# Token-major MLP up units with moving weights, and a turn of the squared rows on TensorE

## The chip, the cores and the metric

The kernel runs on one core of one Trainium2 chip. The metric is the device time of one execution in microseconds. The kernel before takes 2461.74 us (median of 3 runs, 2461.24 to 2465.61).

## What is computed

Two decoder layers over 256 tokens of width 2048, in float32. Layer 0 mixes tokens by attention, layer 1 by a short convolution; each is followed by an MLP of width 8192. Every part is normalised, shifted and scaled, and added back through a gate. The change concerns the MLP alone:

```python
def sq_relu_mlp(h, w_up, w_down):
    return jnp.square(jax.nn.relu(h @ w_up)) @ w_down

for i in range(DEPTH):                       # DEPTH = 2
    ...
    h = modulate(rmsnorm(x, norm_mlp[i]), sh_mlp, sc_mlp)
    x = x + g_mlp[:, None, :] * sq_relu_mlp(h, mlp_w_up[i], mlp_w_down[i])
return rmsnorm(x, final_norm)
```

## The kernel before

**Units.** All large products are cut into units: a 2048 by 512 block of a weight, multiplied with all 256 tokens. A unit has 16 blocks of 128 rows (k), taken as 8 pairs (e = 0 to 7). Each operand is held as two parts in a short float format (fp32r), the rounded value ("hi") and what is left ("lo"), and each product is three matmuls: hi·hi, hi·lo and lo·hi.

**Two ways to multiply a pair.** `chan_pair` (L383) keeps the weight stationary and lets the tokens move: 2 k-blocks by 4 column blocks by 3 products, 24 matmuls of 128x256 (L392 to L394). Channels come out on the partitions, which is how the next product wants them. `tok_pair` (L397) keeps the tokens stationary and lets the weight move: 2 k-blocks by 2 token blocks by 3 products, 12 matmuls of 128x512 (L404 to L406). Tokens come out on the partitions. Up units use `chan_pair`; down units, the value units of the attention and the output projections use `tok_pair`.

**The MLP.** Each layer goes through 4 slices. A slice has 4 up units, whose squared results fill `mid` (16 k-blocks), and 4 down units that multiply `mid`. Slices 1 and 2 of a layer are one loop run twice. There are 32 up units and 32 down units in all. Units alternate between PSUM banks 0, 1 and banks 2, 3; banks 4 to 7 are used by norms, by attention and (bank 7) by the sums of the conditioning vector.

**Queues.** SP loads `raw` a quarter unit at a time. ScalarE rounds it to `w_hi` (`split`, L674), VectorE subtracts to `w_lo` (L1039), both four pairs ahead of TensorE in a ring of four; ScalarE's rounding of step i waits until TensorE has used pair i. Each engine runs its program in order: `body` and `pairs` walk the 8 steps of a unit and call hooks after given steps. In layer 0 VectorE also does the conditioning products `ada` between its steps (L1051), one weight tile per 16 steps, fed by POOL's loads, and TensorE sums each finished tile (`ada_sum`, L440 or L437): two sums in the up units and two in the down units of a slice.

**After an up unit** ScalarE runs `hidden` (L947): Relu out of PSUM into `scratch` (L955, frees the banks), Square in place (L957), Copy to the hi part of `mid` (L959). VectorE's `low_hidden` (L1437) subtracts to the lo part at L1439, after step 0 of the next unit. The first down unit waits for each fourth of `mid` (`mid_chunks`) before its pairs 0, 2, 4 and 6.

**The first unit of a layer's MLP** runs while the norm is still finishing: after each of pairs 0 to 5 TensorE turns 4 blocks of 128x128 (`turn_pair`, L611), and ScalarE and VectorE make the next pair of `h` from them (L924, L762, L1352, L1149), the splits of the weights lying between.

Of the kernel before, what the change touches and what calls it, by code (L numbers as in the profile page):

```python
# [7 lines left out]
ACT = mybir.ActivationFunctionType  # L8
# [3 lines left out]
P = 128  # L12
D = 2048
T = 256
# [9 lines left out]
TT = T // P  # L24
NU = 512
NB = NU // P
NG = D // NU
# [5 lines left out]
SLICES = FF // D  # L33
# [56 lines left out]
def build(nc, x, c, ada_w, ada_b, norm_mix, norm_mlp, fox_w_in, fox_b_f, fox_w_out,  # L90
          conv_w_in, conv_w, conv_w_out, mlp_w_up, mlp_w_down, final_norm, out):
    ctx = ExitStack()
    with ctx:
# [3 lines left out]
        def sem(name):  # L97
            return ctx.enter_context(nc.semaphore(name))
# [18 lines left out]
        mid = sb("mid", [P, KC, 2, T], F32R)  # L117
# [3 lines left out]
        h = sb("h", [P, KC, 2, T], F32R)  # L121
# [13 lines left out]
        scratch = sb("scratch", [P, 2, TT, NU])  # L135
# [6 lines left out]
        ident = sb("ident", [P, P])  # L142
# [27 lines left out]
        ps = ctx.enter_context(nc.psum_tensor("ps", [P, 8, NU], F32))  # L170
# [38 lines left out]
        evacuated = [sem(f"evacuated{i}") for i in range(2)]  # L209
# [31 lines left out]
        added = sem("added")  # L241
        relu = sem("relu")
        relu2 = sem("relu2")
        hid_hi = sem("hid_hi")
        hid_ready = sem("hid_ready")
        conv_zero = sem("conv_zero")
# [132 lines left out]
        def _(pe):  # L379
            mm = nc.tensor.matmul  # L380
            turn = nc.tensor.transpose
# [27 lines left out]
            def pairs(un, src, multiply=chan_pair, ready=None, after=None, es=range(NE)):  # L409
                for e in es:  # L410
                    if e == 0 and not (isinstance(un.u, int) and un.u < 2):
                        pe.wait_ge(evacuated[un.par], un.before)
                    pe.wait_ge(split_ready, NE * un.u + e + 1)
                    if ready is not None:
                        ready(e)
                    multiply(un, e, src).then_inc(split_used, 1)
                    if after is not None and e in after:
                        after[e]()
# [25 lines left out]
            def sums(table, first, n, is_gate, extra=None):  # L444

                hooks = {}
                for e in range(NE):
                    calls = []
                    if NE * n + e in table:
                        i = table[NE * n + e]  # L450
                        calls.append(lambda i=i: ada_sum(first + i, i % 2, is_gate(i)))
                    if extra is not None and e in extra:
                        calls.append(extra[e])
                    if calls:
                        hooks[e] = lambda calls=calls: [f() for f in calls]
                return hooks
# [43 lines left out]
            def h_chunks(i):  # L500
                return lambda e: pe.wait_ge(h_ready, NE * i + e + 1)
# [84 lines left out]
            for u in range(1, 3 * NG):  # L586
                g, t = u // 3, u % 3
                if t == 0:
                    extra = {2: lambda: mix_values(g - 1)}
                elif t == 1:  # L590
                    extra = None if g else {0: forget_logits, 4: forget_turn, 6: forget_sums}
                else:
                    extra = {1 if g else 2: lambda: scores(g), 7: lambda: turn_probs(g)}
# [5 lines left out]
            for n in range(NG):  # L599
                hooks = sums(QKV_SUM, A_START, U_OUT0 + n, qkv_gate, None if n else {2: lambda: mix_values(NG - 1)})  # L600
# [22 lines left out]
            def next_pair(i):  # L623
                return {e: (lambda e=e: turn_pair(i, e + 2)) for e in range(NE - 2)}


            def mlp_slice(base, s, l, first_ada=None, is_gate=False, norm_i=None):
                for n in range(2 * NG):
                    un = at_mlp(base, s, n)
                    extra = next_pair(norm_i) if norm_i is not None and n == 0 else None  # L630
                    hooks = extra if first_ada is None else sums(SLICE_SUM, first_ada, n, lambda i: is_gate, extra)
                    if n < NG:
                        pairs(un, h, ready=h_chunks(norm_i) if norm_i is not None and n == 0 else None, after=hooks)
                        continue
                    ready = mid_chunks(hid_ready, NG * SLICES * l + NG * s) if n == NG else None
                    if n == 2 * NG - 1:
                        by_block(un, mid, after=hooks)
                    else:
                        pairs(un, mid, tok_pair, ready=ready, after=hooks)
# [9 lines left out]
            for i in range(3 * NG):  # L649
                pairs(at(U_CONV + i), h, ready=None if i else h_chunks(2),  # L650
                      after=sums(CONV_SUM, A_CONV, i, lambda i: i < NG, None if i else next_pair(2)))
            for n in range(NG):
                hooks = sums(CONV_SUM, A_CONV, 3 * NG + n, lambda i: i < NG)
# [11 lines left out]
        def _(act):  # L665
# [17 lines left out]
            def body(un, first=None, after=None, last=False):  # L683
                for i in range(NE):
                    if first is not None and i in first:
                        first[i]()
                    if i < WR or not last:
                        split(un.u, i)
                    if after is not None and i in after:
                        after[i]()  # L690
# [242 lines left out]
            def load_gate(layer, part, n_added):  # L933
                act.wait_ge(added, n_added)
                act.dma_start(gate[:, :], ada_b[layer:layer + 1, D * part:D * (part + 1)].broadcast_to([P, D])
                              ).then_inc(gate_arrived, 16)
# [10 lines left out]
            def hidden(un, n, hid, n_added):  # L947

                half = scratch[:, n % 2, :, :]
                flat_half = half.rearrange("p a n -> p (a n)").rearrange("p (j t) -> p j t", j=NB)  # L950
                done(un)
                act.wait_ge(added, n_added)
                if n >= 2:
                    act.wait_ge(hid_ready, hid - 1)
                op(flat_half, un.chan(), ACT.Relu).then_inc(evacuated[un.par], 1)  # L955
                act.wait_ge(evacuated[un.par], un.before + 1)
                op(half, half, ACT.Square).then_inc(relu2, 1)  # L957
                act.wait_ge(relu2, hid + 1)
                op(mid[:, NB * n:NB * (n + 1), 0, :], flat_half, ACT.Copy).then_inc(hid_hi, 1)  # L959

            def mlp_slice(base, s, l, norm_before=None, gate_part=None, norm_after=None, last=False):
                hid = SLICES * NG * l + NG * s
                r0 = (R_MLP0, R_MLP1)[l] + NG * s
                for n in range(NG):
                    un = at_mlp(base, s, n)
                    hooks = {7: lambda: hidden(un, n, hid + n, r0)}
                    if n == 0 and norm_before is not None:
                        hooks.update(rest_of_norm(norm_before))
                        hooks[5] = lambda: load_gate(l, gate_part, r0)
                    body(un, None, hooks)  # L970
                for n in range(NG):
                    final = None
                    if last and n == 0:
                        final = {0: load_final}
                    residual(at_mlp(base, s, NG + n), n, r0, norm_after, final, last=last and n == NG - 1)

            def load_final():
# [54 lines left out]
        def _(dve):  # L1032
# [404 lines left out]
            def low_hidden(n, hid):  # L1437
                dve.wait_ge(hid_hi, hid + 1)
                v.tensor_tensor(mid[:, NB * n:NB * (n + 1), 1, :],  # L1439
                                scratch[:, n % 2, :, :].rearrange("p a n -> p (a n)").rearrange("p (j t) -> p j t", j=NB),  # L1440
                                mid[:, NB * n:NB * (n + 1), 0, :].bitcast(F32), ALU.subtract).then_inc(hid_ready, 1)

            def mlp_slice(base, s, l, i0=None, store=None, norm_before=None, norm_after=None, last=False):
                hid = SLICES * NG * l + NG * s
                r = (R_MLP0, R_MLP1)[l] + NG * s
                for n in range(2 * NG):
                    un = at_mlp(base, s, n)
                    extra = {}
                    if n == 0 and norm_before is not None:
                        extra = rest_of_norm(norm_before)  # L1450
                    if 0 < n <= NG:
                        extra[0] = lambda: low_hidden(n - 1, hid + n - 1)
                    if last and n > NG:
                        extra[1] = lambda: output(n - NG - 1)
                    hooks = extra if store is None else stores(SLICE_STORE, n, store, extra)
                    steps = None if store is None else PLAN_SLICE[0][n]
                    if n < NG:
                        body(un, None, hooks, steps, i0)
                    else:
                        residual(un, n - NG, r, norm_after, hooks, steps, i0, last=last and n == 2 * NG - 1)  # L1460
# [81 lines left out]
```

## Time and profile before

| | |
|---|---|
| median of 3 runs | 2461.74 us (2461.24 to 2465.61) |
| the profiled execution | 2466.71 us, of which its span 2464.7 us |
| TensorE matmul busy | 95% of the span, 15235 matmuls |
| VectorE busy | 69% |
| ScalarE busy | 43% |
| mean granted TensorE clock | 0.972 |
| DMA | 616 MB, 250 GB/s |

A row of a group gives the line, the engine and the operation, what is written and read, the count, the busy time in us and the mean of one in ns. Matmuls are pipelined, so one lasts longer than the distance from start to start, which is what it costs. The timeline gives the start in us from the span's start, and the length.

### The profile page before, as it was taken

What the parts mean: (1) busy time and instruction counts of PE and PEld (TensorE: products, weight loads), DVE (VectorE), ACT (ScalarE), POOL (GpSimd) and SP (SyncE); (2) the same over time, 40 slices, a digit from 0 to 9 for tenths busy, and PEclk for the clock granted to TensorE, in tenths of its full rate; (3) what the DMA queues carried; (4) which work ended last, traced back from release to release, by engine and by line L of the source; (5) the groups of instructions that cost most, each with busy time, mean ns of one, the idle gap of its engine ahead of it and who ended that gap; (6) DMA issues with size and microseconds to landing.
All of it is one profiled execution on the core that took longest, in us unless ns stands there. A gap on an engine that the chain in (4) does not pass through costs nothing.

```text
span 2464.7 us, 36963 instructions
## 1 busy us (share of the span) xinstructions
PE 2352.1 (95%) x15235; PEld 2162.1 (88%) x15235; DVE 1692.3 (69%) x1936; ACT 1051.7 (43%) x1179; POOL 123.9 (5%) x176
## 2 busy tenths in 40 slices
PE   6789999998999999999998999998999999999998
PEld 6779999778989989989988998986998997998996
DVE  5857778886886775776776777765787555455455
ACT  4134434435534533534445333344543443443443
POOL 0000000000000000000000000000000000000000
PEclk9689999999999999999999999999999999999999
DMA  9966778885886886886885788775687555555563
GB/s 364 361 219 222 274 280 301 283 313 183 304 299 228 304 299 211 305 297 227 304 300 164 274 299 290 276 239 169 222 315 248 184 181 190 181 185 189 190 205 120
DMA packets 267568, 616.17 MB, mean 250 GB/s; under 512 B 11672, under 2 KB 12040, under 8 KB 266512
## 3 DMA queue, kind: packets, MB, share of 16 engines
q1 hardware_dynamic: 219968, 437.29, 52.5%
q0 software_dynamic: 43520, 167.78, 18.7%
q10 hardware_dynamic: 3920, 8.75, 1.0%
q8 instruction: 126, 2.06, 0.3%
q14 instruction: 34, 0.28, 0.0%
HBM read 611.66 MB, written 2.13 MB: 249 GB/s over the span
## 4 chain that ended last, share of the span: by engine, by line
PE 85%; DVE 7%; ACT 3%; DMA 2%; issue 2%; SPq 0%; ACTq 0%; DVEq 0%
PE ps L392 16%; PE ps L393 15%; PE ps L394 15%; PE ps L404 11%; PE ps L406 11%; PE ps L405 11%; DVE acc L1051 2%; DMA ada_raw<-in_ada_w_dram 2%; DVE w_lo L1039 2%; ACT w_hi L674 1%; DMA start_ring<-in_ada_w_dram 1%; PE ps L440 1%; PE ps L471 1%; PE ps L437 1%; ACT scratch L820 1%
## 5 line engine op out<-in xcount | busy, mean ns | idle before, releaser
L1039 DVE TENSOR_TENSOR w_lo<-raw,w_hi 128x1024 fp32r<-128x1024 f32 x768 | 938.3, 1223 | 614.0 <-ACT w_hi L674 610.5
L674 ACT ACTIVATE w_hi<-raw 128x1024 fp32r<-128x1024 f32 x760 | 802.9, 1059 | 1180.8 <-PE ps L394 645.7
L392 PE MATMUL ps<-h,w_hi 128*128 128x256 f32 x3328 | 960.8, 289 | 12.2 <-DVE h L1149 9.0
L393 PE MATMUL ps<-h,w_hi 128*128 128x256 f32 x3328 | 951.4, 286 | 2.4 <-issue 2.4
L394 PE MATMUL ps<-h,w_lo 128*128 128x256 f32 x3328 | 950.7, 286 | 0.0
L392 PEld LDWEIGHTS ps<-h,w_hi 128*128 128x128 f32 x3328 | 649.0, 195 | 17.8 <-issue 16.1
L393 PEld LDWEIGHTS ps<-h,w_hi 128*128 128x128 f32 x3328 | 649.1, 195 | 5.3 <-issue 5.1
L394 PEld LDWEIGHTS ps<-h,w_lo 128*128 128x128 f32 x3328 | 648.6, 195 | 0.0
L404 PE MATMUL ps<-w_hi,mid 128*128 128x512 f32 x1280 | 503.1, 393 | 0.0
L405 PE MATMUL ps<-w_hi,mid 128*128 128x512 f32 x1280 | 498.7, 390 | 0.0
L406 PE MATMUL ps<-w_lo,mid 128*128 128x512 f32 x1280 | 498.6, 390 | 0.0
L1051 DVE SCALAR_TENSOR_TENSOR acc<-ada_raw,ca,acc 128x512 f32<-128x512 f32 x600 | 448.6, 748 | 26.0 <-DMA ada_raw<-in_ada_w_dram 18.5
L405 PEld LDWEIGHTS ps<-w_hi,mid 128*128 128x128 f32 x1280 | 240.7, 188 | 51.5 <-issue 2.2
L404 PEld LDWEIGHTS ps<-w_hi,mid 128*128 128x128 f32 x1280 | 240.8, 188 | 51.1 <-issue 1.2
L406 PEld LDWEIGHTS ps<-w_lo,mid 128*128 128x128 f32 x1280 | 240.6, 188 | 50.3
L373 POOL DMA_DIRECT2D ada_raw<-in_ada_w_dram x160 | 120.0, 750 | 1744.1 <-DVE acc L1051 1713.2
L1051 DVE SCALAR_TENSOR_TENSOR acc<-start_ring,ca,acc 128x512 f32<-128x512 f32 x88 | 66.1, 751 | 6.5 <-DMA start_ring<-in_ada_w_dram 3.7
L471 PE MATMUL ps<-ca,start_ring 128*128 128x1 f32 x256 | 46.8, 312 | 13.4 <-DMA start_ring<-in_ada_w_dram 7.8
L471 PEld LDWEIGHTS ps<-ca,start_ring 128*128 128x128 f32 x256 | 46.7, 280 | 14.0 <-DMA start_ring<-in_ada_w_dram 8.2
L404 PE MATMUL ps<-w_hi,h 128*128 128x512 f32 x128 | 50.3, 393 | 0.0
L405 PE MATMUL ps<-w_hi,h 128*128 128x512 f32 x128 | 49.9, 390 | 0.0
L406 PE MATMUL ps<-w_lo,h 128*128 128x512 f32 x128 | 49.9, 390 | 0.0
(166 smaller groups left out, 985.4 us busy)
## 6 DMA issues: line engine op xcount, KB each, us to landing
ada_raw<-in_ada_w_dram POOLq DMA_DIRECT2D x160, 1024.0 KB, 7.3
raw<-in_mlp_w_up_dram SPq DMA_DIRECT2D x128, 1024.0 KB, 5.4
raw<-in_mlp_w_down_dram SPq DMA_DIRECT2D x128, 1024.0 KB, 5.2
raw<-in_fox_w_in_dram SPq DMA_DIRECT2D x48, 1024.0 KB, 5.5
raw<-in_conv_w_in_dram SPq DMA_DIRECT2D x48, 1024.0 KB, 6.1
start_ring<-in_ada_w_dram SPq DMA_DIRECT2D x32, 1024.0 KB, 10.7
raw<-in_fox_w_out_dram SPq DMA_DIRECT2D x16, 1024.0 KB, 6.6
raw<-in_conv_w_out_dram SPq DMA_DIRECT2D x16, 1024.0 KB, 5.2
```

The costliest lines, as they stand in the source:

```text
L373: pool.dma_start(ada_raw[:, t % 2], ada_quarter(A_START + t // NQ, t % NQ)).then_inc(ada_arrived[t % 2], 16)
L392: mm(o, hi[:, jc], xh, start=(k == 0 and j % 2 == 0), stop=False, skip_group_check=True)
L393: mm(o, hi[:, jc], xl, start=False, stop=False, skip_group_check=True)
L394: last = mm(o, lo[:, jc], xh, start=False, stop=(k == KC - 1), skip_group_check=True)
L404: mm(o, xh, hi, start=(k == 0), stop=False)
L405: mm(o, xl, hi, start=False, stop=False)
L406: last = mm(o, xh, lo, start=False, stop=(k == KC - 1))
L437: last = mm(ps[:, SUM, :], ones[:, :], acc[:, slot, :], start=True, stop=True)
L471: last = mm(ps[:, 6 + i % 2, j:j + 1], start_ring[:, t % RING, k % QK, P * j:P * (j + 1)], ca[:, k:k + 1], start=(k == START_DVE and j == ...
L674: op(w_hi[:, e % WR], raw[:, e // 2, EK * (e % 2):EK * (e % 2 + 1)], ACT.Copy).then_inc(hi_ready, 1)
L1039: v.tensor_tensor(w_lo[:, e % WR], raw[:, e // 2, EK * (e % 2):EK * (e % 2 + 1)], w_hi[:, e % WR].bitcast(F32), ALU.subtract).then_inc(spl ...
L1051: v.scalar_tensor_tensor(acc[:, slot, :], src, ca[:, col:col + 1], acc[:, slot, :], ALU.mult, ALU.add).then_inc(steps, 1)
```

## The change

Up units call `tok_pair` in place of `chan_pair`, so that tokens come out on the partitions. ScalarE's Relu and Square work on that layout. TensorE then turns the squared rows, 8 blocks of 128x128, into banks 4 and 5 (`turn_hidden`), in the next unit after pair 2. ScalarE rounds the hi part of `mid` out of those banks (`round_hidden`), and VectorE subtracts its lo part out of them, both after step 3 of the next unit in place of straight after the Square and after step 0. `scratch` is free again once it is turned, so `hidden` waits for `hid_turned`. `turn_hidden` waits for the Square (`relu2`) and for the lo part of the unit before (`hid_ready`).

```diff
+            def turn_hidden(n, hid):
+
+                pe.wait_ge(relu2, hid + 1)
+                pe.wait_ge(hid_ready, hid)
+                for j in range(NB):
+                    for a in range(TT):
+                        last = turn(ps[:, 4 + j // 2, T * (j % 2) + P * a:T * (j % 2) + P * (a + 1)],
+                                    scratch[:, n % 2, a, P * j:P * (j + 1)], ident[:, :])
+                last.then_inc(hid_turned, 1)
+
             def mlp_slice(base, s, l, first_ada=None, is_gate=False, norm_i=None):
                 for n in range(2 * NG):
                     un = at_mlp(base, s, n)
                     extra = next_pair(norm_i) if norm_i is not None and n == 0 else None
+                    if 0 < n <= NG:
+                        extra = {2: lambda: turn_hidden(n - 1, NG * SLICES * l + NG * s + n - 1)}
                     hooks = extra if first_ada is None else sums(SLICE_SUM, first_ada, n, lambda i: is_gate, extra)
                     if n < NG:
-                        pairs(un, h, ready=h_chunks(norm_i) if norm_i is not None and n == 0 else None, after=hooks)
+                        pairs(un, h, tok_pair, ready=h_chunks(norm_i) if norm_i is not None and n == 0 else None, after=hooks)
                         continue
...
                 half = scratch[:, n % 2, :, :]
-                flat_half = half.rearrange("p a n -> p (a n)").rearrange("p (j t) -> p j t", j=NB)
                 done(un)
                 act.wait_ge(added, n_added)
                 if n >= 2:
-                    act.wait_ge(hid_ready, hid - 1)
-                op(flat_half, un.chan(), ACT.Relu).then_inc(evacuated[un.par], 1)
+                    act.wait_ge(hid_turned, hid - 1)
+                op(half, un.tok(), ACT.Relu).then_inc(evacuated[un.par], 1)
                 act.wait_ge(evacuated[un.par], un.before + 1)
                 op(half, half, ACT.Square).then_inc(relu2, 1)
-                act.wait_ge(relu2, hid + 1)
-                op(mid[:, NB * n:NB * (n + 1), 0, :], flat_half, ACT.Copy).then_inc(hid_hi, 1)
+
+            def round_hidden(n, hid):
+                act.wait_ge(hid_turned, hid + 1)
+                op(mid[:, NB * n:NB * (n + 1), 0, :], ps[:, 4:6, :].rearrange("p b (j t) -> p (b j) t", t=T),
+                   ACT.Copy).then_inc(hid_hi, 1)
...
+                    if n:
+                        hooks[3] = lambda: round_hidden(n - 1, hid + n - 1)
...
+                    if n == 0:
+                        final[3] = lambda: round_hidden(NG - 1, hid + NG - 1)
...
             def low_hidden(n, hid):
                 dve.wait_ge(hid_hi, hid + 1)
                 v.tensor_tensor(mid[:, NB * n:NB * (n + 1), 1, :],
-                                scratch[:, n % 2, :, :].rearrange("p a n -> p (a n)").rearrange("p (j t) -> p j t", j=NB),
+                                ps[:, 4:6, :].rearrange("p b (j t) -> p (b j) t", t=T),
                                 mid[:, NB * n:NB * (n + 1), 0, :].bitcast(F32), ALU.subtract).then_inc(hid_ready, 1)
...
                     if 0 < n <= NG:
-                        extra[0] = lambda: low_hidden(n - 1, hid + n - 1)
+                        extra[3] = lambda: low_hidden(n - 1, hid + n - 1)
```

## Rows read from the trace of the kernel before

**Rows 1.** The page: engine totals over the span, and the chain that ended last.
```profile
PE 2352.1 (95%) x15235; PEld 2162.1 (88%) x15235; DVE 1692.3 (69%) x1936; ACT 1051.7 (43%) x1179; POOL 123.9 (5%) x176
PE 85%; DVE 7%; ACT 3%; DMA 2%; issue 2%; SPq 0%; ACTq 0%; DVEq 0%
```
**Rows 2.** Stretches: length, busy us (count) by engine, granted clock, DMA share, GB/s.
```profile
1960.05:1983.09 23.04, 23.04 (x194) 23.04 (x193) 10.85 (x9) 11.39 (x12) 0.00 (x0) 1.00 0.57 184
...
617.78:665.56 47.78, 47.78 (x386) 46.60 (x385) 37.94 (x43) 22.83 (x24) 4.49 (x6) 1.00 0.89 313
...
1724.50:1729.80 5.30, 5.26 (x25) 5.29 (x26) 3.71 (x5) 1.81 (x4) 0.00 (x0) 0.50 0.03 3
...
31.00:47.00 16.00, 14.53 (x71) 14.47 (x71) 13.18 (x18) 8.99 (x13) 0.00 (x0) 1.00 1.05 387
```
**Rows 3.** Waits of TensorE, 590 to 1200 us and 1830 to 2380 us.
```profile
PE ps L393 <- issue: 2.4, 1, 2.4
```
```profile
PE ps L392 <- issue: 2.5, 1, 2.5
```
**Rows 4.** Timeline of ScalarE in an up unit, then in a down unit.
```profile
1996.53 1.06 ACT L674 ACTIVATE w_hi<-raw 128x1024 fp32r<-128x1024 f32 x1 [1.82 <-PE ps L394]
1999.41 1.06 ACT L674 ACTIVATE w_hi<-raw 128x1024 fp32r<-128x1024 f32 x1 [1.82 <-PE ps L394]
...
2016.07 1.06 ACT L674 ACTIVATE w_hi<-raw 128x1024 fp32r<-128x1024 f32 x1 [1.66 <-PE ps L406]
2018.79 1.06 ACT L674 ACTIVATE w_hi<-raw 128x1024 fp32r<-128x1024 f32 x1 [1.66 <-PE ps L406]
```
**Rows 5.** Timeline of TensorE, layer 1's first up unit: the matmuls that follow four turns.
```profile
1736.85 0.36 PE L392 MATMUL ps<-h,w_hi 128*128 128x256 f32 x1
...
1740.16 0.36 PE L392 MATMUL ps<-h,w_hi 128*128 128x256 f32 x1
```
**Rows 6.** Timeline of TensorE in the attention: twelve turns in a row.
```profile
206.39 0.27 PE L566 MATMUL ps<-ident,scratch 128*128 128x128 f32 x1
...
207.49 0.31 PE L567 MATMUL ps<-ident,scratch 128*128 128x128 f32 x1
207.51 0.50 PE L392 MATMUL ps<-h,w_hi 128*128 128x256 f32 x1
```
**Rows 7.** Timeline of TensorE at the start: eight turns of x.
```profile
33.28 1.94 PE L496 MATMUL ps<-ident,scratch 128*128 128x128 f32 x8 [1.47 <-ACT scratch L741]
```
**Rows 8.** Timeline of TensorE in a down unit: eight sums between pairs.
```profile
919.33 0.95 PE L440 MATMUL ps<-ones,acc 128*128 128x1 f32 x8
920.13 0.49 PE L404 MATMUL ps<-w_hi,mid 128*128 128x512 f32 x1
920.46 0.40 PE L405 MATMUL ps<-w_hi,mid 128*128 128x512 f32 x1
```
**Rows 9.** Timeline of VectorE and ScalarE, layer 1's first up unit, from one pair of h to the next.
```profile
1744.57 0.54 DVE L1352 TENSOR_SCALAR hb<-ps,gain,mod 128x256 f32<-128x256 f32 x1
...
1746.76 1.23 DVE L1039 TENSOR_TENSOR w_lo<-raw,w_hi 128x1024 fp32r<-128x1024 f32 x1 [0.26 <-ACT w_hi L674]
1747.90 0.54 DVE L1352 TENSOR_SCALAR hb<-ps,gain,mod 128x256 f32<-128x256 f32 x1
```
```profile
1745.14 0.63 ACT L762 ACTIVATE h<-hb 128x512 fp32r<-128x512 f32 x1 [0.77 <-DVE hb L1352]
1745.68 1.04 ACT L674 ACTIVATE w_hi<-raw 128x1024 fp32r<-128x1024 f32 x1
```
**Rows 10.** Groups by line, ScalarE and VectorE.
```profile
L1039 DVE TENSOR_TENSOR w_lo<-raw,w_hi 128x1024 fp32r<-128x1024 f32 x768 | 938.3, 1223 | 614.0 <-ACT w_hi L674 610.5
L1051 DVE SCALAR_TENSOR_TENSOR acc<-ada_raw,ca,acc 128x512 f32<-128x512 f32 x600 | 448.6, 748 | 26.0 <-DMA ada_raw<-in_ada_w_dram 18.5
...
L1239 DVE TENSOR_TENSOR mid<-ps,mid 128x1024 fp32r<-128x1024 f32 x4 | 4.9, 1218 | 0.0
...
L830 ACT ACTIVATE mid<-ps 128x1024 fp32r<-128x1024 f32 x4 | 4.0, 1008 | 0.0
```

More of the change, by code:

```diff
@@ L243, in build @@
         relu2 = sem("relu2")
+        hid_turned = sem("hid_turned")
         hid_hi = sem("hid_hi")
@@ L969, in mlp_slice @@
                         hooks[5] = lambda: load_gate(l, gate_part, r0)
+                    if n:
+                        hooks[3] = lambda: round_hidden(n - 1, hid + n - 1)
                     body(un, None, hooks)
                 for n in range(NG):
-                    final = None
+                    final = {}
+                    if n == 0:
+                        final[3] = lambda: round_hidden(NG - 1, hid + NG - 1)
                     if last and n == 0:
-                        final = {0: load_final}
+                        final[0] = load_final
                     residual(at_mlp(base, s, NG + n), n, r0, norm_after, final, last=last and n == NG - 1)
```

## The prediction

> **What bounds the kernel now.** I read the engine totals first, then the chain that ended last, then stretches of single units, and last the timeline inside them. TensorE is busy in 95% of the span and carries 85% of the chain [rows 1]. An average over stages doesn't say what a unit is bound by, so the stretches decide: an up unit of layer 1 lasts 23.04 us with TensorE busy for all 23.04, VectorE for 10.85 and ScalarE for 11.39; two up units of layer 0 last 47.78 us with TensorE busy for 47.78 and VectorE for 37.94 [rows 2]. TensorE's only wait in each MLP loop is one of 2.4 to 2.5 us, at the jump back [rows 3]. So in the MLP the time is the number of TensorE instructions by their distance from start to start. What the others do is free as long as it stays inside their slack.
>
> The distance is read from ScalarE, whose split starts each time TensorE has used a pair: 2.88 us for a pair of an up unit, 2.72 us for a pair of a down unit [rows 4]. That is 24 matmuls of 256 columns at 120 ns, and 12 of 512 columns at 227 ns. The columns at 2.4 GHz would take 106.7 and 213.3 ns, so either kind carries 13.3 ns beside its columns, and the up unit pays it twice as often. 8 x 2.88 = 23.04 is the whole unit.
>
> **The matmuls.** The up units change from 24 to 12 matmuls per pair over the same columns. Down units have exactly the new form, and the value units of the attention have it with the same stationary `h`, so I take 2.72 us: 0.16 us less per pair, 1.28 us per unit. It would be 41.0 us for 32 units, if each were bound by TensorE.
>
> Two aren't, the first unit of each layer's MLP. There a chain passes through VectorE's modulation (starts 1744.57), ScalarE's rounding of h (1745.14), ScalarE's split (1745.68), VectorE's split (1746.76) and the next modulation (1747.90): 3.33 us around [rows 9], against 3.31 us that TensorE takes for a pair and four turns (1736.85 to 1740.16) [rows 5]. Taking 0.16 us from TensorE leaves the 3.33. I give these two units 0.2 us each, for the pairs after the last turn; the bounds are 0 and 1.28. Saved: 30 x 1.28 + 2 x 0.2 = 38.8 us.
>
> **The turns.** 32 x 8 turns are added, all on the engine that bounds. Three rows bound them. Four turns between pairs of the same MLP cost 3.31 - 2.88 = 0.43 us, the restart of the matmuls included [rows 4, 5]. In a row of twelve, ten steps take 1.10 us, 0.11 each, and the first matmul follows the last turn by 0.02 [rows 6]. Eight then cost 0.43 + 4 x 0.11 = 0.87 us. At the kernel's start eight took 1.94 us [rows 7]. I take the low end, because its rows lie in the very stage that is changed. Matmuls of 512 columns surround them now. After eight short sums in a down unit the second matmul follows the first by 0.33 us where 0.227 is usual, 0.10 lost in the restart [rows 8]; part of such a loss is in the 0.43 already. I add 0.02 us (bounds 0 and 0.10). So 0.89 us, and 32 x 0.89 = 28.5 us. An up unit becomes 8 x 2.72 + 0.89 = 22.65 us in place of 23.04.
>
> A rule of the Trainium skill speaks against this, in the page "TensorE: Matmul & The Clock Gate", Part 4 (PE-mode transpose): a transpose in a kernel's context takes about 275 ns. As an estimate by that page, eight would be 2.2 us, a unit 0.92 us slower than before, and the kernel 2491 us. The trace doesn't agree as to distance: the rows show 0.11 us from turn to turn.
>
> **The sums of layer 0.** Eight of them lie in up units whose matmuls are now long: the restart after them loses up to the same 0.10 us more than it did [rows 8]. I book 0.5 us in all (0 to 0.8).
>
> **ScalarE.** The Copy to `mid` is of the same size and reads PSUM now, which takes 1008 ns [rows 10], so nothing is added, and it moves from the end of the unit to after step 3. Its split of step 0 comes 1 us earlier. ScalarE is half idle (11.39 of 23.04), which hides all of it. Its new wait (`hid_turned` before the rounding) stands behind split 3, which itself waits until TensorE has finished pair 3; the turns come before pair 3 in TensorE's order, so it is met by then. Nothing queues behind it.
>
> **VectorE.** The subtraction is of the same size and reads PSUM: 1218 ns [rows 10]. It moves from step 0 to step 3. In layer 0 VectorE is busy for 37.94 of 47.78 us; that becomes about 38 of 47.0. It stays under TensorE.
>
> **The new waits on TensorE.** `turn_hidden` waits for the Square. That is done about 3.1 us after the unit's end (a split, the Relu and the Square, about 1.05 us each by rows of this size [rows 4, 10]), and the turns are due after three pairs, 8.2 us. 5 us are left. It also waits for the lo part of the unit before, done a unit ago. Queued behind are pairs 3 to 7, with the ring of splits four pairs ahead.
>
> The last up unit of a slice is the tight one, since the first down unit needs its lo part before pair 6. From that unit's start: pair 3 ends at 4 x 2.72 + 0.89 = 11.8; ScalarE's split ends at 12.8 and its rounding at 13.8; VectorE's split ends at 14.1 and the lo part at 15.3; pair 6 starts at 6 x 2.72 + 0.89 = 17.2. Slack 1.9 us in layer 1. In layer 0 up to two conditioning steps of 0.75 us can stand ahead, which leaves 0.4. Before, the lo part came after step 0. So the change costs nothing here, but has little to spare.
>
> **DMA, SP and POOL** get no new transfer. The rate rises by 1.7% at most where TensorE is faster; the DMA share was 0.89 in the densest units [rows 2]. Loads of `raw` are issued about 6 pairs (16 us) ahead of their split. Free, with the smallest reserve in layer 0.
>
> **The loop's jump.** Two waits of 2.4 to 2.5 us for instructions stay [rows 3]. Before them now stand matmuls that run longer, which could hide 0.3 us of each; I book nothing.
>
> **Where the clock is low** (0.50 granted in the stretch after the norm [rows 2], which is the level of 1.2 GHz), 25 instructions fill 5.3 us: 213 ns for 256 columns, no more than the columns. The short form pays nothing there, so the long one gains nothing. That concerns one or two pairs per norm, already outside the sum.
>
> **The sum.** -38.8 + 28.5 + 0.5 = -9.8 us. The profiled execution took 2466.71 us (span 2464.7 and 2.0 around it); it becomes about 2456.9. It stood 5.0 us above the median of the runs, within what a few more microseconds of low clock can do. From the median: 2461.7 - 9.8 = 2451.9, I say 2452 us.
>
> **Rivals.**
> A, the slower one: a turn costs what it did at the start, 1.94 us for eight [rows 7]. For it: that stretch has 1.00 in the clock column [rows 2], so the row isn't excused by the clock; and nothing shows turns of `scratch` between 512-column matmuls. Against: the turns of [rows 5, 6] ran at 0.11. It decides above 1.28 / 8 = 0.16 us per turn. Time: 2461.7 - 38.8 + 62.1 + 0.5 = 2485.5 us.
> B, also slower: the 13.3 ns isn't a cost per matmul in the up units, so that a long one there takes 2 x 120 ns. Then nothing is saved: 2461.7 + 28.5 + 0.5 = 2490.7 us. Against: the long matmuls of the down units keep 227 ns [rows 4]. A page of the Trainium skill comes out near this by another road: "TensorE: Matmul & The Clock Gate", Back-to-back issue gap, gives N / 2.4 + 2.5 ns. As an estimate by it, a pair would shrink by 0.03 us only, and the kernel would take about 2483 us. The 120 and 227 ns of this trace disagree with it by 11 ns each, and the measurement decides.
> C: the fourth chunk comes late. It eats more than its 0.4 us in layer 0's four slices by one or two VectorE instructions (0.75 to 1.22 us): 2452 + 4 x 1.5 = 2458 us.
> D: the change doesn't reach layer 0, because VectorE's and DMA's load there sets the pace once TensorE is faster. Only 16 units gain: 2457 us. Against: 38 of 47.0 us.
> E: instruction waits or stretches of low clock fall otherwise, 3 to 8 us more: 2455 to 2460 us.
>
> **How the numbers follow.** Forecast 0.78 (own range 2447 to 2456), C 0.05, D 0.06, E 0.04, A 0.04, B 0.03. About 0.2% (4.9 us) is what a measurement of this kernel can tell from no change, so faster means below 2456.8. Forecast and half of E give 0.80 faster; C, D and the rest of E 0.13; A and B 0.07. The range reaches from 2446 (all 32 units gain in full, turns 0.86, part of the jump hidden) to 2460 (C, D and E); A and B are left out.
>
> **What the profile after should show.** Splits in up units 2.72 us apart; 8 turns from pair 2 to pair 3 taking 0.89 us; layer 1's units 22.65 us from Relu to Relu; 15235 - 32 x 96 + 256 = 12419 matmuls; no wait of TensorE for `mid` in a first down unit. A turn above 0.16 us, pairs above 2.77 us, or a wait before pair 6 would make me wrong.

## The result and the profile after

The changed kernel takes 2440.37 us (median of 4 runs, 2438.44 to 2442.30) beside 2461.97 us of the kernel before: ratio 0.9914, 95% interval 0.9897 to 0.9931. That is 21.6 us less where 9.8 were forecast, and 5.6 us below the range. Measured once more it took 2443.77 us (6 runs) beside 2461.16 us (21 runs), ratio 0.9928 (0.9908 to 0.9947). The direction was right; the forecast was about half of the change.

The page of the changed kernel: engine totals, the instruction queue, and the chain that ended last.

```profile
span 2436.5 us, 31379 instructions
PE 2331.3 (96%) x12419; PEld 2017.1 (83%) x12419; DVE 1694.6 (70%) x1936; ACT 1047.3 (43%) x1179; POOL 124.3 (5%) x176
q8 instruction: 94, 1.54, 0.3%
PE 88%; DVE 5%; ACT 3%; issue 2%; DMA 1%; SPq 0%; ACTq 0%; DVEq 0%
```

TensorE carries more of the chain than before [rows 1], with 12419 matmuls as counted. The costliest new groups (the turns, the rounding, the subtraction), as groups by line and shape:

```profile
L1458 DVE TENSOR_TENSOR mid<-ps,mid 128x1024 fp32r<-128x1024 f32 x32 | 39.0, 1217 | 0.0
L634 PE MATMUL ps<-ident,scratch 128*128 128x128 f32 x256 | 33.1, 272 | 0.0
L973 ACT ACTIVATE mid<-ps 128x1024 fp32r<-128x1024 f32 x32 | 32.3, 1009 | 0.0
```

One up unit of layer 1, then two of layer 0, as stretches; they answer to the first two of [rows 2].

```profile
1939.13:1961.79 22.66, 22.66 (x106) 18.85 (x105) 10.94 (x9) 11.27 (x13) 0.00 (x0) 1.00 0.59 187
607.92:655.08 47.16, 47.16 (x214) 38.46 (x213) 38.22 (x44) 22.53 (x24) 4.51 (x6) 1.00 0.92 319
```

22.66 us was forecast as 22.65, and the two of layer 0 as about 47.0. TensorE is still busy for all of it. ScalarE in that unit of layer 1 shows the moved rounding 11.8 us after the Relu, behind split 3, where it was put in the sum (12.8 us after the unit's start, the Relu being at 1.1):

```profile
1939.13 1.01 ACT L967 ACTIVATE scratch<-ps 128x1024 f32<-128x1024 f32 x1
1940.18 1.06 ACT L969 ACTIVATE scratch<-scratch 128x1024 f32<-128x1024 f32 x1
...
1950.91 1.01 ACT L973 ACTIVATE mid<-ps 128x1024 fp32r<-128x1024 f32 x1
```

So the units did what the prediction says. What it doesn't have is at the loops' jumps: the profile shows no wait of TensorE in the changed kernel between 586 and 1212 us or between 1735 and 2352 us, where before had one of 2.4 to 2.5 us in each layer [rows 3]. I measure the jump by the distance from the last Relu of one slice to the first Relu of the next. The stretch that holds the jump takes 114.96 us before and 111.83 after in layer 0, and 114.53 and 109.69 in layer 1; the same stretch one slice later, without a jump, takes 112.32 and 111.81, 110.09 and 109.69. So the jump cost 2.6 and 4.4 us, and now costs nothing.

### The profile page after: what moved, and what is told of

The parts are those of the page before. It is cut to its first block, busy times and chain, and to the rows that moved or that the text cites. A ratio compares the mean times of both kernels' runs of the same rounds, so it can differ in the third digit from the quotient of the medians.

```text
span 2436.5 us, 31379 instructions
## 1 busy us (share of the span) xinstructions
PE 2331.3 (96%) x12419; PEld 2017.1 (83%) x12419; DVE 1694.6 (70%) x1936; ACT 1047.3 (43%) x1179; POOL 124.3 (5%) x176
## 4 chain that ended last, share of the span: by engine, by line
PE 88%; DVE 5%; ACT 3%; issue 2%; DMA 1%; SPq 0%; ACTq 0%; DVEq 0%
PE ps L405 22%; PE ps L407 22%; PE ps L406 22%; PE ps L393 6%; PE ps L395 6%; PE ps L394 6%; DVE acc L1070 1%; DVE w_lo L1058 1%; PE ps L634 1%; ACT w_hi L687 1%; DMA start_ring<-in_ada_w_dram 1%; PE ps L441 1%; PE ps L472 1%; PE ps L438 1%; ACT scratch L833 1%
## 5 line engine op out<-in xcount | busy, mean ns | idle before, releaser
L405 PE MATMUL ps<-w_hi,h 128*128 128x512 f32 x1152 | 456.6, 396 | 4.3 <-DVE h L1168 4.3
L407 PE MATMUL ps<-w_lo,h 128*128 128x512 f32 x1152 | 450.6, 391 | 0.0
L406 PE MATMUL ps<-w_hi,h 128*128 128x512 f32 x1152 | 450.1, 391 | 0.0
L393 PE MATMUL ps<-h,w_hi 128*128 128x256 f32 x1280 | 373.4, 292 | 5.9 <-DVE h L1168 5.4
L394 PE MATMUL ps<-h,w_hi 128*128 128x256 f32 x1280 | 367.7, 287 | 0.0
L395 PE MATMUL ps<-h,w_lo 128*128 128x256 f32 x1280 | 367.6, 287 | 0.0
L405 PEld LDWEIGHTS ps<-w_hi,h 128*128 128x128 f32 x1152 | 217.5, 189 | 50.9 <-issue 6.8
L393 PEld LDWEIGHTS ps<-h,w_hi 128*128 128x128 f32 x1280 | 251.9, 197 | 8.2 <-issue 7.4
L407 PEld LDWEIGHTS ps<-w_lo,h 128*128 128x128 f32 x1152 | 217.2, 189 | 46.3
L406 PEld LDWEIGHTS ps<-w_hi,h 128*128 128x128 f32 x1152 | 217.5, 189 | 44.6 <-issue 1.0
L394 PEld LDWEIGHTS ps<-h,w_hi 128*128 128x128 f32 x1280 | 251.8, 197 | 1.5 <-issue 1.5
L395 PEld LDWEIGHTS ps<-h,w_lo 128*128 128x128 f32 x1280 | 251.3, 196 | 0.0
```

The lines of the kernel that those rows point to most:

```text
L393: mm(o, hi[:, jc], xh, start=(k == 0 and j % 2 == 0), stop=False, skip_group_check=True)
L394: mm(o, hi[:, jc], xl, start=False, stop=False, skip_group_check=True)
L395: last = mm(o, lo[:, jc], xh, start=False, stop=(k == KC - 1), skip_group_check=True)
L405: mm(o, xh, hi, start=(k == 0), stop=False)
L406: mm(o, xl, hi, start=False, stop=False)
L407: last = mm(o, xh, lo, start=False, stop=(k == KC - 1))
```

## The experiments

The theory after the result (J, for jump): the units give what the sum said, and 7 us more come from the jumps. Its rival U: the units gain more than the traces of single units suggest. If J holds, why is the wait gone: because the matmuls behind the jump are longer (form), because the body is shorter (size), or because it lies elsewhere among the blocks by which instructions are fetched (place)?

### The loops written out

```diff
-            with pe.Fori(1, SLICES - 1) as s:
+            for s in range(1, SLICES - 1):
```

In the kernel before:

> The kernel before with TensorE's two MLP loops written out (slices 1 and 2 of each layer one after the other), all else as it was. Theory J (the missing term is the loop's jump): in the trace of before the jump back costs 2.6 us in layer 0 and 4.4 us in layer 1 (wait for instructions, and in layer 1 a stretch of low clock behind it), and the changed kernel has no wait there. Then this kernel takes about 7 us less than before, 2455 us, and has no wait for instructions in the MLP. Rival U (the units gained more than the sum said, the jump is small change or moves elsewhere): within 2 us of before, 2460 to 2464 us.

Measured: 2449.96 us (4 runs, beside 2459.74 us of before), ratio 0.9951 (0.9935 to 0.9968). The two stretches with the jump take 112.14 and 110.09 us. J stands, U falls: the kernel before becomes 9.8 us faster, where 7 were expected, without any change to its arithmetic.

In the changed kernel:

> The changed kernel with the same two loops of TensorE written out. Theory J: nothing is left at the jump of the changed kernel, so this takes the same, 2440 us within 2 us; and the distance to the kernel before written out is what the units alone give, 10 to 15 us. Rival U: the distance between the two written-out kernels stays at about 21 us.

Measured: 2444.45 us, ratio 0.9933 (0.9916 to 0.9949), 2 us above the expected 2440 within 2; the stretches with the jump take 111.74 and 109.69 us, as in the changed kernel. The distance between the two written-out kernels is 5.5 us, below the 10 to 15 expected and far from U's 21. Their traces (6.3 us apart) say where it went: from the first Relu of a layer's MLP to its last it is 5.1 us less in layer 0 and 5.5 us less in layer 1, and the last turns behind each give back 0.87 us, so the units gain 8.8 us. The changed one reaches its first Relu 1.6 us later and loses another 0.9 us between the MLPs, where the code of both is the same.

### Old and new up units mixed

The switch is a set of unit numbers, here for the up unit's multiplication on TensorE; ScalarE and VectorE follow it.

```diff
-                        pairs(un, h, tok_pair, ready=...
+                        pairs(un, h, tok_pair if n in TOK else chan_pair, ready=...
```

TOK = (1, 2, 3):

> The changed kernel, but up unit 0 of each slice as before (stationary weights, no turns); up units 1 to 3 as changed. The loop's body is 1896 and 1856 TensorE instructions, against 2418 and 2378 before and 1722 and 1682 after. Why the jump costs nothing in the changed kernel has two explanations. Form: the first matmuls behind the jump are long, so the queue lasts until the instructions come. Then here, where they are short again, the wait of about 2.4 us is back at both jumps. Size: the shorter body is still held when the loop jumps back. Then no wait here if the limit lies above 1896. By the units alone: two of eight are bound by the norm's chain anyway and lose their turns, six lose 0.37 us each: 2440 + 2 - 1.5 = 2441 us; with the wait back 2446 to 2448 us.

Measured: 2445.47 us, ratio 0.9940 (0.9924 to 0.9957). The wait is partly back. Timeline of TensorE at layer 0's jump; what stands in brackets is the wait:

```profile
925.25 0.28 PE L395 MATMUL ps<-h,w_hi 128*128 128x256 f32 x1
...
925.97 0.28 PE L395 MATMUL ps<-h,w_hi 128*128 128x256 f32 x1
927.65 0.28 PE L396 MATMUL ps<-h,w_hi 128*128 128x256 f32 x1 [1.40 <-issue]
```

Seven matmuls run, then 1.40 us pass. In layer 1 there is one of 0.58 us at the jump and one of 0.32 us behind 27 matmuls (the expectation of the moved kernel, below, counts 28). Neither form (2.4 us at both) nor size says that.

TOK = (0, 1):

> The changed kernel, but up units 2 and 3 of each slice as before; units 0 and 1 as changed, so that long matmuls stand behind the jump. The body is 2070 instructions in layer 0 and 2030 in layer 1. Form: no wait at either jump. Size: the wait is back at one or both, if the limit lies below them (2048 instructions would be 128 KiB at 64 bytes each, a guess that would part the two layers). By the units alone 16 x 0.37 = 6 us more than the changed kernel: 2446 us; with waits back up to 2453 us.

Measured: 2451.14 us (6 runs), ratio 0.9962 (0.9949 to 0.9975), and no wait for instructions at either jump, though the body is longer than in the kernel before it. A body longer than the one that waited doesn't wait, so size alone doesn't decide. Of the 7 us above the changed kernel (2443.8 us when run again, below), the 16 old units are 5 to 6 (0.70 us per slice of layer 1, 178.42 against 177.72); the rest stands in the attention, which is 3 us longer in this trace than in that of the changed kernel run again.

### The kernel before once more, and shifted

> The kernel before, unchanged, once more, as a control for the profiles. The trace that the prediction rests on holds about 9 us before the end of the first up unit that the changed kernel's doesn't, in the attention, whose code is the same in both: one stretch of 32.2 us between two marks that takes 27.3 us in the changed kernel, one of 8.8 that takes 7.3. Scatter theory: that was this one execution, and here the stretches take 27.3 to 28.3 and 7.3 us; the jumps in the MLP keep their 2.4 us waits, and the span is 2457 to 2462 us. Rival theory (the change helps the attention too, by the place of its code or otherwise): 32 and 8.8 us again.

Measured: 2459.6 us (10 runs), ratio 0.9994 (0.9982 to 1.0007); the profiled one has a span of 2456.5 us. The long stretch of the attention takes 27.5 us here. In the trace of the prediction it had this row, a wait for VectorE that was itself late by a transfer, and low clock behind it (0.56 granted from 350 to 355 us), the level of 1.2 GHz:

```profile
346.58 1.05 PE L440 MATMUL ps<-ones,acc 128*128 128x1 f32 x8 [1.50 <-DVE acc L1051]
```

Of the other eleven traces three have a wait of 0.5 to 0.7 us there, eight have none, and that stretch is within 1 us the same in all eleven. The other stretch, 8.8 against 7.3 us, turns up in one trace of the changed kernel as well. So both are scatter. The waits at the jumps are there again:

```profile
PE ps L393 <- issue: 2.7, 1, 2.7
```
```profile
PE ps L392 <- issue: 2.5, 1, 2.5
```

The shift puts waits that are long met, two at a time, ahead of the pairs of slice 0 of each layer (`pad[0]` is 2 there and 0 elsewhere):

```diff
                 for e in es:
+                    for _ in range(pad[0]):
+                        pe.wait_ge(const_ready, 11)
```

> The kernel before with 60 extra TensorE instructions (waits that are long met) ahead of each MLP loop, so that everything behind them lies 60 and 120 instructions further on. Nothing else changes. Place theory (the wait at the jump depends on where the target lies in the blocks by which instructions are fetched): the waits change or vanish, up to 7 us less. Form or size theory: 2.4 to 2.5 us at both jumps again, time as before.

Measured: 2452.38 us (8 runs), ratio 0.9966 (0.9951 to 0.9980), 8.8 us less than before where up to 7 were expected. The waits are gone at both jumps (stretches of 112.22 and 110.09 us). Matmuls, body and its length are those of the kernel before; only the place differs. So neither form nor size is needed to explain the waits of the kernel before. What size does in the changed kernel the instruction queue shows further on.

### The turns alone

> The kernel before with the eight turns of each up unit added on TensorE at the same place (after pair 2 of the next unit), and their result unused; everything else as before, short matmuls included. Prices the turns alone. By the prediction 0.87 us per unit among short matmuls: an up unit 23.04 + 0.87 = 23.91 us in layer 1, 28 us in all, about 2488 us. Rival A of the prediction (1.94 us per unit): 62 us, 2522 us. The loop's body grows to 2490 and 2450 instructions and its first matmuls stay short: by form and by size alike the waits at the jumps stay.

Measured: 2478.88 us, ratio 1.0066 (1.0041 to 1.0091). One up unit of layer 1:

```profile
1967.46:1991.36 23.90, 23.90 (x202) 23.90 (x201) 10.85 (x9) 11.38 (x13) 0.00 (x0) 1.00 0.55 178
```

0.86 us for eight turns among short matmuls, forecast 0.87. The time is 9 us less than expected, and 7 of these are the jumps: the code is longer, so the bodies moved, and the waits are gone here too.

```diff
-                for j in range(NB):
-                    for a in range(TT):
+                for j in range(NB - 1, NB):
+                    for a in range(TT - 1, TT):
                         last = turn(...)
```

> The changed kernel with one turn of the eight left, the last, which signals; the other seven are left out, so most of the hidden layer isn't what the reference has. Prices the turns among long matmuls. By the prediction 0.11 us each: an up unit of layer 1 goes from 22.68 to 21.90 us, 32 x 7 x 0.11 = 25 us in all, 2417 us. By rival A (0.24 each): 54 us, 2388 us. No wait at the jumps by the place theory (the bodies start at 210 and 248 of a block, behind place 203).

Measured: 2416.95 us, ratio 0.9828 (0.9803 to 0.9854), and no wait at the jumps. The changed kernel, measured beside other runs of before, has 0.9914 and 0.9928, so this is 21 to 25 us less, where 25 were expected.

```profile
1925.27:1947.17 21.90, 21.90 (x99) 18.09 (x98) 10.94 (x9) 11.27 (x12) 0.00 (x0) 1.00 0.59 192
```

Seven turns among long matmuls are worth 22.66 - 21.90 = 0.76 us, 0.11 each. Rival A falls.

### The changed kernel once more, and moved to the old place

> The changed kernel once more, on the same chip and beside the same runs of before, for a narrower ratio. The units and the jumps alone give 8.6 + 7.2 = 16 us: 2461.7 - 16 = 2446 us, ratio 0.9935. The first measurement gave 0.9914, 0.9897 to 0.9931. Scatter theory: the ratio here lies between the two, 0.992 to 0.994. Rival (something else gains 5 us): 0.991 again, with the interval below 0.993.

Measured: ratio 0.9928 (0.9908 to 0.9947), where scatter put it. 0.991 isn't excluded by the interval. The two profiled ones of this and of before have spans of 2440.2 and 2456.5 us, 16.3 apart, which the accounting below closes.

`fill[0]` starts at 376 and at 100 ahead of the two loops; two waits become one instruction in the compiled stream, which makes 188 and 50.

```diff
+                    for _ in range(min(8, fill[0])):
+                        pe.wait_ge(const_ready, 11)
+                        fill[0] -= 1
```

> The changed kernel with TensorE instructions that do nothing (waits long met) ahead of both MLP loops, 188 and 50 of them, so that the first instruction of each loop's body comes to lie where it lay in the kernel before: at 198 in a block of 256 instructions (16 KB), by the compiled instruction streams. There it was at 198 and 196, and the wait came after 1 and 3 matmuls; in the kernel with the first up unit old it was at 185 and 147, and the waits (1.4 and 0.3 us) came after 7 and 28 matmuls: all four end near place 203. Place theory: the changed kernel now waits about 2.3 us for instructions after 1 to 3 long matmuls of each loop's second pass, with or without low clock behind: 4.6 to 7 us more than the changed kernel's 2442, that is 2447 to 2449 us. Rival (form: long matmuls cover the fetch wherever the loop lies, or the change took the wait away): no wait, 2442 us.

Measured: 2449.86 us (10 runs), ratio 0.9966 (0.9952 to 0.9980). Layer 0, then layer 1:

```profile
925.64 0.50 PE L405 MATMUL ps<-w_hi,h 128*128 128x512 f32 x1
928.40 0.50 PE L406 MATMUL ps<-w_hi,h 128*128 128x512 f32 x1 [2.27 <-issue]
```
```profile
2075.75 0.39 PE L405 MATMUL ps<-w_hi,h 128*128 128x512 f32 x1
2075.98 0.39 PE L406 MATMUL ps<-w_hi,h 128*128 128x512 f32 x1
2078.27 0.50 PE L407 MATMUL ps<-w_lo,h 128*128 128x512 f32 x1 [1.91 <-issue]
```

The stretches with the jump grow from 112.03 and 109.69 us to 114.72 and 111.90, 4.9 us together; that lies in the 4.6 to 7 us expected. The medians are 6.1 us apart, and the rest isn't in the MLPs of the traces. The wait was put into the changed kernel by moving its loops, at both jumps.

## Why the prediction was wrong

The kernels in the order of where the loops' bodies begin within a block of 256 instructions (by the compiled streams), and what TensorE did behind the jump:

| kernel | layer 0: place, wait | layer 1: place, wait |
|---|---|---|
| before | 198, 2.4 us after 1 matmul | 196, 2.5 us after 3 |
| after, moved to 198 | 198, 2.3 us after 1 | 198, 1.9 us after 2 |
| first up unit old | 185, 1.4 us after 7 | 147, 0.6 us at the jump, 0.3 us after 27 |
| last two old | 104, none | 78, none |
| before, shifted | 2, none | 60, none |
| after; before with turns | 10, none | 216, none |
| after, one turn | 210, none | 248, none |

A matmul is two instructions, and three others stand between the place where a body begins and its first matmul. So the first instruction that had to wait lies at 203 and 205 (before), 203 and 205 (after, moved) and 202 and 205 (first up unit old): there the next block had not come. I read the block's end off these waits; why it lies there and not at 256 of the compiled stream no run shows. The further before that place the body begins, the longer TensorE has work and the shorter the wait. That the blocks are of 256 instructions the instruction queue shows too: the TensorE streams of the two written-out kernels are 30714 and 25114 instructions long, 120.0 and 98.1 times 256, and the queue moved 120 and 98 packets of 16.4 KB each.

```profile
q8 instruction: 120, 1.97, 0.3%
```
```profile
q8 instruction: 98, 1.61, 0.3%
```

The packets' times show the wait at work. In the four traces that have waits (before, before once more, first up unit old, after moved) a packet starts 0.1 to 1.6 us behind the first matmul after the jump, and each of the eight waits that follow a matmul ends 2.2 to 2.6 us after the start of such a packet. The packet ahead of these starts 2.6 to 3.1 us before that first matmul, and costs nothing. The exception is the wait of 0.58 us right at one jump: there that packet took 2.0 us, against 0.9 to 1.4 elsewhere, which may be its cause but isn't shown to be.

They also show what happens in the changed kernel. In layer 0 its body is fetched again for the second pass, as in the kernel before (packets 3.0 us before and 0.3 us behind the jump), and there is no wait because TensorE has work until the block comes. In layer 1 nothing is fetched: the queue moves no packet between 2051 and 2257 us, the whole second pass, where the moved kernel has nine between 2072 and 2240 us. By the compiled streams, with blocks that end at 203, this body of 1683 instructions touches 7 blocks from place 216 and 8 from place 198; layer 0's, of 1755, touches 8 from either place. Both bodies of the kernel with one turn touch 7, and neither is fetched again. Every body that touches 8 blocks or more is. So size isn't out of it: layer 1 of the changed kernel has no wait because a shorter body at a good place needs no fetch, layer 0 because of the place alone.

The Trainium skill, page "Runtime: NRT & Kernel Launch", Instruction fetch mechanics, states that fetch goes in 16 KiB blocks of 256 instructions and is sequential, and that a taken branch to a place outside what is held costs a fetch before execution goes on. The traces agree as to the blocks and that a jump can cost a fetch. They differ as to where it costs: behind the target's own block (only 0.58 us, once, stood at the target itself). The price hangs on where in its block the target lies, between 0 and 2.7 us of waiting here.

**Step by step.**

- *What bounds the kernel*: right. TensorE was and is busy in every up unit.
- *The matmuls*: right. An up unit of layer 1 takes 22.65 to 22.69 us (forecast 22.65).
- *The first units of a layer*: right, with 0.2 us too much booked for each. From the first modulation of VectorE to the first Relu the written-out pair takes 30.69 and 30.74 us in layer 0, and 31.49 us both times in layer 1. TensorE now waits longer for the chain there, 2.2 us in layer 1 against 1.8 us before.
- *The turns*: right, 0.86 us measured among short matmuls, 0.11 us each among long ones. The 275 ns that the Trainium skill gives ("TensorE: Matmul & The Clock Gate", Part 4, as cited in the prediction) are close to the duration of a turn here (272 ns, the group of L634), not to its distance; for the cost of a turn the measured 0.11 us decides.
- *The sums of layer 0*: right in size. An up unit with a sum takes 23.61 us, 0.92 more than one without, against 0.88 before: 0.3 to 0.4 us in all.
- *ScalarE, VectorE, the new waits*: right. No wait of TensorE for `mid` or the Square. Rivals C and D fall: layer 0's units gain 0.3 us each, as TensorE allows.
- *The loop's jump*: this step failed. The prediction saw the waits, "Two waits of 2.4 to 2.5 us for instructions stay", and costed a change in them at nothing, since it asked only what stands before the jump. It didn't ask what the wait hangs on, which is the place of the body and how many blocks it touches. Nor did it count the low clock behind layer 1's wait, which made 4.4 us of 2.5: after TensorE had stood still for 2.45 us, 3.1 us at 0.50 granted, the 1.2 GHz level, from 2087.08 us on in the control. The term was booked at 0 and measured 7.0 us.

```profile
2087.08 0.58 PE L392 MATMUL ps<-h,w_hi 128*128 128x256 f32 x1 [2.45 <-issue]
```
```profile
2087.08:2090.20 3.12, 3.12 (x14) 3.12 (x15) 0.69 (x1) 0.00 (x0) 0.00 (x0) 0.50 0.72 229
```

- *The range*: its low end allowed "part of the jump hidden", 0.3 us each. By its own terms that end is 2461.7 - 41.0 + 27.5 - 0.6 = 2447.6 us, not 2446. With both jumps gone, the sum gives 2461.7 - 9.8 - 7.0 = 2445 us, below the range already. E held the opposite sign only (3 to 8 us more).

**The accounting**, by the two traces taken again (2456.5 and 2440.2 us): start and attention, to layer 0's first Relu, +1.1; layer 0's MLP from first to last Relu -8.0, of which the jump 2.6; its last down units and the convolution -0.4, with 0.87 us of the last turns in them; layer 1's MLP -9.9, of which the jump 4.4; the rest +0.9, the last turns again. Sum -16.3. The units alone (the two MLPs without the jumps, and the last turns) are -9.1 in this pair and -8.8 in the written-out pair; 9.8 was forecast.

**What stays open.** The first measurement shows 21.6 us, the second 17.4 (13 to 23 by its interval), the mechanisms 16. The traces differ by up to 5 us before the first Relu (the one that the prediction rests on by up to 10) and by up to 3 us between the MLPs, where the code is the same, and I take the rest for that scatter; but the first interval (0.9897 to 0.9931) starts at 17 us, a little above 16, so it isn't shown that nothing else helps. The 5.5 us between the written-out pair agree with its traces (8.8 less 2.5 of such scatter); whether those 2.5 us are chance no run shows. The cause of the 0.58 us right at one jump is open too.

## What to carry to other kernels

A kernel that is bound by one engine can be summed from its distances between starts, and here the sum held to 1 us for 32 units. But any change in the number of instructions also moves every loop behind it, and a loop's jump cost 0 to 4.4 us here by its place and by the blocks that its body touches. Look at the wait for instructions behind each jump, and at the packets of the instruction queue there, before crediting or blaming a change of that size, and compare with the loops written out.

## What the runs showed of the hardware

The wait behind a jump back is set by where the target lies in its block of 256 instructions: 1.9 to 2.7 us with 5 to 7 instructions left before place 203, 1.4 us with 18, 0.3 us with 56, and none at the other places run. It ends 2.2 to 2.6 us after the start of a packet of the instruction queue. A body that touched 7 such blocks was not fetched again for its second pass (four jumps in three traces), one of 8 or more was (all sixteen others). In layer 1 of the kernel before the wait of 2.45 us was followed by 3.1 us of low clock (0.50 granted, the 1.2 GHz level); the 1.9 to 2.7 us waits at the other jumps were followed by 1.00. Matmuls of this type follow each other by 120 ns for 256 columns and 227 ns for 512 at 2.4 GHz, 13.3 ns more than their columns, and by 213 ns for 256 at 1.2 GHz, their columns alone. A turn of a float32 128x128 block costs 0.11 us from start to start in a busy stream.
